# The order of long and short matmuls inside a piece: eight and eight in place of two and two

## The reference

```python
# layer 0: pooling mixer and gated linear recurrence
u = rms_norm(x, g) @ w_in_even          # 2048 -> 6144
x = x + concat([y_a, y_b]) @ w_out_even # 2048 -> 2048
# layer 1: stick-breaking attention
u = rms_norm(x, g) @ w_in_odd           # 2048 -> 8192
x = x + (att * silu(gate)) @ w_out_odd  # 2048 -> 2048
# behind each mixer
q = rms_norm(x, gx) @ wq                # 2048 -> 2048
k, v = split(rms_norm(mem, gm) @ wkv)   # 2048 -> 4096
x = x + softmax(q k^T / sqrt(512)) v @ wo
```

## Time and profile before

| | us |
|---|---|
| median of 3 runs | 1656.75 |
| lowest and highest | 1656.69, 1656.75 |
| the profiled execution | 1656.68 |
| its span, from the first to the last instruction | 1654.9 |
| TensorE busy in the span, matmuls | 1639.2 |
| TensorE weight loads | 1436.1 |
| VectorE busy | 1172.3 |
| ScalarE busy | 797.1 |
| GpSimd busy | 183.8 |

### The profile page before, as it was taken

One profiled execution on the slowest core, in us unless ns is written; L12 is line 12 of the kernel. 1 busy time (PEld: TensorE's weight loads), 2 busy tenths in 40 slices (PEclk: granted clock), 3 DMA queues, 4 the chain that ended last, 5 costly groups with the idle time before them and its releaser, 6 DMA issues.

```text
span 1654.9 us, 26963 instructions
## 1 busy us (share of the span) xinstructions
PE 1639.2 (99%) x9752; PEld 1436.1 (87%) x9752; DVE 1172.3 (71%) x1281; ACT 797.1 (48%) x940; POOL 183.8 (11%) x126
## 2 busy tenths in 40 slices
PE   9999999999999999999999999999999999999998
PEld 7888888888888888888888888888888888888887
DVE  7856697777776787767765567777667777677664
ACT  6633434465554455445433345555555554455432
POOL 0000060000003310043100000000000013400042
PEclk9999999999999999999999999999999999999999
DMA  9666755555555554457666665556556555554363
GB/s 311 199 190 184 229 175 175 175 170 164 165 166 179 186 172 148 140 178 229 187 184 193 188 189 177 166 165 189 158 186 185 171 175 189 180 166 152 121 199 112
DMA packets 291059, 296.50 MB, mean 179 GB/s; under 512 B 9024, under 2 KB 288704, under 8 KB 291008
## 3 DMA queue, kind: packets, MB, share of 16 engines
q1 hardware_dynamic: 290864, 295.73, 57.4%
q10 hardware_dynamic: 144, 0.07, 0.0%
HBM read 293.68 MB, written 2.10 MB: 179 GB/s over the span
## 4 chain that ended last, share of the span: by engine, by line
PE 96%; DVE 2%; DMA 1%; ACT 1%; issue 1%; DVEq 0%; ACTq 0%
PE ps L256 60%; PE ps L259 30%; PE ps L339 1%; PE ps L320 1%; DVE wpair L793 0%; PE ps L465 0%; PE ps L480 0%; PE ps L379 0%; DMA raw<-xa_wkv 0%; PE ps L472 0%; PE ps L330 0%; PE ps L402 0%; DMA xkT<-mem 0%; PE ps L434 0%; PE ps L429 0%
## 5 line engine op out<-in xcount | busy, mean ns | idle before, releaser
L531 ACT ACTIVATE wpair<-raw 128x1024 fp32r<-128x1024 f32 x544 | 574.9, 1059 | 702.3 <-PE ps L259 694.9
L793 DVE TENSOR_TENSOR wpair<-raw,wpair 128x1024 fp32r<-128x1024 f32 x544 | 700.7, 1300 | 285.8 <-ACT wpair L531 282.9
L256 PE MATMUL ps<-xpair,wpair 128*128 128x512 f32 x1920 | 607.1, 397 | 0.0
L256 PE MATMUL ps<-ypair,wpair 128*128 128x512 f32 x1536 | 483.3, 396 | 3.2 <-DVE wpair L793 1.9
L259 PEld LDWEIGHTS ps<-xpair,wpair 128*128 128x128 f32 x1920 | 360.6, 188 | 85.2
L259 PE MATMUL ps<-xpair,wpair 128*128 128x256 f32 x1920 | 377.8, 278 | 0.0
L259 PEld LDWEIGHTS ps<-ypair,wpair 128*128 128x128 f32 x1536 | 288.5, 188 | 68.2
L259 PE MATMUL ps<-ypair,wpair 128*128 128x256 f32 x1536 | 301.9, 278 | 0.0
L256 PEld LDWEIGHTS ps<-xpair,wpair 128*128 128x128 f32 x1920 | 292.9, 189 | 1.4 <-issue 0.6
L256 PEld LDWEIGHTS ps<-ypair,wpair 128*128 128x128 f32 x1536 | 233.8, 189 | 4.1 <-issue 4.1
L256 PE MATMUL ps<-wpair,ypair 128*128 128x512 f32 x512 | 160.8, 395 | 0.0
(11 more groups left out here) (180 smaller groups left out, 939.7 us busy)
## 6 DMA issues: line engine op xcount, KB each, us to landing
raw<-xa_wkv SPq DMA_DIRECT2D x128, 512.0 KB, 4.0
raw<-w_in_odd SPq DMA_DIRECT2D x128, 512.0 KB, 3.9
raw<-w_in_even SPq DMA_DIRECT2D x96, 512.0 KB, 3.6
raw<-xa_wq SPq DMA_DIRECT2D x64, 512.0 KB, 3.5
raw<-xa_wo SPq DMA_DIRECT2D x64, 512.0 KB, 3.4
raw<-w_out_even SPq DMA_DIRECT2D x32, 512.0 KB, 3.8
raw<-w_out_odd SPq DMA_DIRECT2D x32, 512.0 KB, 4.3
xkT<-mem SPq DMA_DIRECT2D x8, 512.0 KB, 6.6
```

The costliest lines, as they stand in the source:

```text
L256: mm(ps[:, 2 * parity + j, :], still[:, k, 0, j * P:(j + 1) * P], move[:, k].rearrange("p h n -> p (h n)"), start=(k == 0), stop=False)
L531: fn(wpair[:, KP * p:KP * (p + 1), 0, :], raw[:, p], ACT.Copy).then_inc(hi_ready, 1)
L793: v.tensor_tensor(wpair[:, kp, 1, :], raw[:, p], wpair[:, kp, 0, :].bitcast(F32), ALU.subtract).then_inc(lo_ready, 1)
```

## The change

One line is added in `piece`. The loop over the four k-tiles of a piece is written twice: the first goes through them with the long matmuls, the second with the short ones. Nothing else is changed: the same 16 matmuls with the same operands, banks and flags, the waits ahead of them, and the signal on the last one, which is the short one of the last k-tile and the second bank in both. Python unrolls these loops when the program is built. From line 258 on, the lines of the kernel move down by one.

```diff
--- before.py
+++ after.py
@@ -255,6 +255,7 @@
                     for j in range(2):
                         mm(ps[:, 2 * parity + j, :], still[:, k, 0, j * P:(j + 1) * P],
                            move[:, k].rearrange("p h n -> p (h n)"), start=(k == 0), stop=False)
+                for k in range(KP * p, KP * (p + 1)):
                     for j in range(2):
                         last = mm(ps[:, 2 * parity + j, S:2 * S], still[:, k, 1, j * P:(j + 1) * P], move[:, k, 0],
                                   start=False, stop=(k == KT - 1))
```

## The result

The changed kernel takes **1659.38 us** (median of 20 runs, 1659.21 to 1660.23) against 1656.75 us (20 runs, 1656.62 to 1657.48): a ratio of 1.0016, 95% interval 1.001 to 1.0022. That is 2.6 us more, within the 0.2% that the prediction called no difference, while it had forecast +8.8 us.

A forecast was written before the change was run, and what follows sets the result against it. The prediction took TensorE's steady stream of long and short matmuls as the bound. Shorts in a row added +8.8 us, longs and waits nothing, so 1656.7 us became 1665.5 us (+0.5%), range 1637 to 1675.

The forecast's parts named there:

- no difference: Whole kernel: a time change under 0.2%, 3.3 us or 6 ns per piece; chance 0.30.
- wrong in kind: Sign in the profile after: a long's time moves by more than 3 ns, or TensorE waits for VectorE's weights inside a stage.
- Short matmuls in a row: Eight shorts of a piece: six pay 117.9 instead of 115.2 ns, +16.2 ns per piece, +8.8 us.
- The nearer row: Cross-attention runs of 24 short matmuls, 117.9 ns each, taken as nearest to the changed shorts; another line's run gave 120.0.
- Long matmuls in a row: Eight longs of a piece: each stays at 233.1 ns, no change; ends -54.8 us and +6.2 us.
- Faster, 1637.4: Rival on the eight longs: uniform runs have 11.2 instead of 19.8 ns surplus; -19.3 us; faster case's chance 0.25.
- Order makes no difference, 1656.7: Rival on the shorts: alternating two banks keeps them at 115.2 ns, so the time stays 1656.7 us; chance 0.30.
- Back-to-back issue gap: Skill rule for the matmul stream: N/2.4 + 2.5 ns whatever stands before; a four takes 650 ns, this change nothing.
- LDWEIGHTS (loading the stationary operand): Skill rule for weight loads: columns/1.2, an estimate of 107 ns, so a run of shorts has no slack for its loads.
- the likeliest case: Matmuls of a piece: shorts in a row cost more and longs don't change, 1660 to 1675 us; chance 0.45.

The follow-up runs named there:

- sixteen in a row: Against the kernel before: sixteen long, then sixteen short matmuls, across the end of a piece; 1655.68 us, ratio 0.9994; again 1655.53 us, 0.9992.
- at four: Against the kernel before: four long and four short matmuls, twice a piece; 1663.27 us, ratio 1.0039.
- at one: Against the kernel before: one long and one short matmul, always in turn; 1669.24 us, ratio 1.0078.
- all long: Against the changed kernel: low times high left out, the long products made twice, so all sixteen matmuls of a piece are long; 2107.28 us.
- narrow shorts: Two kernels, against the changed kernel: short matmuls stream 192 or 128 of their 256 columns; 1624.82 us with 192, 1637.14 us with 128.
- 384 columns: Against the changed kernel: long matmuls, except those of a chunk's first k-tile, stream 384 of their 512 columns; 1485.18 us.

## Why the prediction was wrong

Right was what bounds the kernel and what doesn't: TensorE's waits moved by 0.7 us in all, the other engines' idle time covered them, and the time changed in the main by the stream of matmuls. A change of 6.7 ns a piece x 544 is 3.6 us, of which 2.6 came; the periods of a chunk that hold other products took less than a third of their part. The sign that the prediction had named for being wrong in kind, a long's time moving by more than 3 ns, came: the settled ones moved by 6.4 ns, the mean of the eight by 3.0.

- **Short matmuls in a row**: the mechanism was right and the term mis-sized. I took 117.9 ns from six of them, +16.2 ns a piece. Measured are 113.3, 119.1 and six of 120.0, together 952.4 ns against 921.6 (8 x 115.2): **+30.8 ns**. The nearer row was the dearer one, 120.0, which I kept for a bound. The argument for the other, that it reads alternating operands, was no measurement.
- **Long matmuls in a row**: this step failed. "I take 233.1, because it is this very instruction" put nothing there. Measured are 1840.9 ns against 1864.8 for eight: **-23.9 ns**, -13.0 us over 544 pieces. The evidence of the earlier trace rows, that the second of two is no faster than the first, was true on average (233 and 236, then 233 and 231 ns start to start) and worth nothing: the long ones need five to settle, so a pair can't show it. The two terms give +30.8 - 23.9 = +6.9 ns, and the periods 6.7.
- **Faster, 1637.4**: this rival's mechanism was the right one for the long ones, that in a run they have the surplus which a short one has in a run. It had the surplus at 11.2 ns where it is 13.3, and it left out that the first five pay for the change of kind. With 13.3 for all six that it counted, it would have had -38.4 instead of -51.6 ns.
- **Order makes no difference, 1656.7**: nearest to the time, and for a wrong reason. The bank plays no part, and the near balance is of two changes of 24 and 31 ns.
- **The rules of the Trainium skill** ("TensorE: Matmul & The Clock Gate"). That of "Back-to-back issue gap", columns/2.4 + 2.5 ns, is given there for the gap of an isolated matmul, and the section adds that in a stream with weight loads both set the spacing; the prediction took it as a rule for the stream, and it doesn't hold for this one: measured are 13.3 in place of 2.5 in a settled run, and up to 28 behind a change of kind. That of "LDWEIGHTS (loading the stationary operand)", columns/1.2, an estimate of 107 ns a load, pointed to the right side; the floor measured here is 112 ns, and full shorts are not on it.
- The range, 1637 to 1675, holds the result. The chance of 0.30 for no difference was too low beside 0.45, since the likeliest case priced the cost alone; with both at their measured size they nearly cancel.

Left open: why a change from short to long costs what it does, and why it depends on the width and on the run before. Counted for each change and the way back, it is 20 ns above the settled sum both at eight and at sixteen in a row, so it hangs on the change there and not on the number of matmuls; at four it is 13.3 or 16.7, at two 3.3 (above the settled sum it is 13.3 ns a piece at two and two, 20.0 at eight, 10.0 at sixteen, 26.7 or 33.3 at four, 0 or 53.3 at one). Nor is 13.3 ns the surplus of every run of this type and width: the 24 equal matmuls of the earlier trace rows stay at 117.9 ns in one place and 113.7 in another, with 256 columns as well. What selects between two patterns of one order was seen (the stream's last break) but not explained.

## What to carry to other kernels

In a stream like this one, where TensorE hardly ever waits, the order of its matmuls still has a price, of some ns each, and it couldn't be read from pairs: make one kernel with a single kind in a row to have the settled durations, and one with the change of kind at another distance. A pattern's own period, taken over tens of its repetitions, is the number to compare. Runs of one kind that are longer than the five or so that a long one takes to settle are not enough: here four and eight cost and sixteen pays, because it has half the changes of eight, and the gain is under 0.1%.

## What was not expected of the hardware

- Every repeating period is a whole number of steps of 6.67 ns, 16 cycles of TensorE at 2.4 GHz: 418 steps a piece at two and two, 419 at eight, 835 for two pieces at sixteen, 420 or 421 at four, 416 or 424 in turn, 544 with all long, 408 and 412 with the narrow shorts, 351 with 384 columns. The loss of this change is one step a piece.
- The same instructions in the same order run at 2773.3 or at 2826.7 ns a piece for a hundred us and more. The pattern changed only where the stream was broken; what decides which one follows wasn't found.
- The f32 matmuls of the earlier trace rows, each record with a load of its own too, take 216.3 ns a record. If a record stands for 512 columns' time, which no row shows, their surplus is 3.0 ns and not 13.3. What makes the difference wasn't tried.
- Back to back, weight loads of 128 columns start 112 ns apart, and a run of narrower matmuls makes the next wide one pay for their being late (252 and 283 ns instead of 233).
